# FFN up products from the fifth step on: one 512-column matmul for the weights' high half against both halves of the operand

## The reference

```python
def swiglu(h, w13, w2):
    gate, up = jnp.split(h @ w13, 2, axis=-1)
    return (jax.nn.silu(gate) * up) @ w2
...
        x = x + 0.5 * swiglu(rms_norm(x, ffn1_norm[l]), ffn1_w13[l], ffn1_w2[l])
...
        x = x + 0.5 * swiglu(rms_norm(x, ffn2_norm[l]), ffn2_w13[l], ffn2_w2[l])
```

## Time and profile before

| | |
|---|---|
| median of three runs | 1532.71 us (1531.86 to 1532.9) |
| the profiled execution | 1531.94 us, its span 1530.2 us |
| TensorE matmuls | 1494.6 us busy (98%), 11618 instructions |
| VectorE | 1164.2 us busy (76%), 1645 instructions |
| ScalarE | 788.5 us busy (52%), 1135 instructions |
| POOL | 115.6 us busy (8%), 71 instructions |
| DMA | 311.02 MB, 203 GB/s over the span |

### The profile page before, as it was taken

One profiled execution on the slowest core, in us unless ns is written; L12 is line 12 of the kernel. 1 busy time (PEld: TensorE's weight loads), 2 busy tenths in 40 slices (PEclk: granted clock), 3 DMA queues, 4 the chain that ended last, 5 costly groups with the idle time before them and its releaser, 6 DMA issues.

```text
span 1530.2 us, 28532 instructions
## 1 busy us (share of the span) xinstructions
PE 1494.6 (98%) x11618; PEld 1436.2 (94%) x11618; DVE 1164.2 (76%) x1645; ACT 788.5 (52%) x1135; POOL 115.6 (8%) x71
## 2 busy tenths in 40 slices
PE   7999999999999999999989999999999999899998
PEld 7999998999999899999769999987699999899998
DVE  7887788888877868887767876774778987785564
ACT  6534458654435644445765443454654544564442
POOL 0013000000200102110000100000000111000000
PEclk9999999999999999999999999999999999999999
DMA  7676752646675547675232867643345887345540
GB/s 271 244 256 235 250 218 84 246 172 244 236 259 192 220 158 283 243 252 220 84 138 111 303 244 251 247 148 137 104 152 216 303 283 255 128 149 217 186 166 28
DMA packets 44566, 311.02 MB, mean 203 GB/s; under 512 B 5744, under 2 KB 6000, under 8 KB 7344
## 3 DMA queue, kind: packets, MB, share of 16 engines
q1 hardware_dynamic: 42048, 303.33, 54.5%
q0 software_dynamic: 1840, 5.20, 1.1%
q10 hardware_dynamic: 576, 1.05, 0.2%
HBM read 308.46 MB, written 1.05 MB: 202 GB/s over the span
## 4 chain that ended last, share of the span: by engine, by line
PE 77%; DVE 3%; ACT 1%; issue 0%; DVEq 0%; ACTq 0%
PE psum L1860 21%; PE psum L1866 21%; PE psum L1867 21%; PE psum L2065 3%; PE psum L2071 3%; PE psum L2070 3%; DVE w_lo L1072 1%; PE psum L2382 1%; PE psum L2393 0%; PE psum L2312 0%; PE psum L2277 0%; PE psum L2184 0%; ACT w_hi L515 0%; DVE buf L1579 0%; PE psum L2232 0%
## 5 line engine op out<-in xcount | busy, mean ns | idle before, releaser
L1860 PE MATMUL psum<-u_hi,w_hi 128*128 128x256 f32 (+1 forms) x2288 | 654.9, 286 | 18.2 <-DVE u_lo L1169 9.7
L1072 DVE TENSOR_TENSOR w_lo<-raw,w_hi 128x1024 fp32r<-128x1024 f32 x480 | 593.9, 1254 | 93.4 <-ACT w_hi L515 93.2
L1866 PE MATMUL psum<-u_lo,w_hi 128*128 128x256 f32 (+1 forms) x2288 | 648.8, 284 | 0.0
L1867 PE MATMUL psum<-u_hi,w_lo 128*128 128x256 f32 (+1 forms) x2288 | 648.6, 283 | 0.0
L515 ACT ACTIVATE w_hi<-raw 128x1024 fp32r<-128x1024 f32 x480 | 488.4, 1047 | 73.6 <-PE psum L1860 58.7
L1860 PEld LDWEIGHTS psum<-u_hi,w_hi 128*128 128x128 f32 x2288 | 439.2, 192 | 22.8 <-DVE w_lo L1072 9.9
L1866 PEld LDWEIGHTS psum<-u_lo,w_hi 128*128 128x128 f32 x2288 | 439.4, 192 | 0.4
L1867 PEld LDWEIGHTS psum<-u_hi,w_lo 128*128 128x128 f32 x2288 | 439.3, 192 | 0.0
L1860 PE MATMUL psum<-hid_hi,w_hi 128*128 128x256 f32 x1220 | 346.0, 284 | 1.2 <-issue 1.2
L1866 PE MATMUL psum<-hid_lo,w_hi 128*128 128x256 f32 x1220 | 345.2, 283 | 0.0
L1867 PE MATMUL psum<-hid_hi,w_lo 128*128 128x256 f32 x1220 | 345.2, 283 | 0.0
(11 more groups left out here) (258 smaller groups left out, 1017.9 us busy)
## 6 DMA issues: line engine op xcount, KB each, us to landing
raw<-stream SPq DMA_DIRECT2D x288, 1024.0 KB, 4.8
buf<-tab POOLq DMA_DIRECT2D x2, 768.0 KB, 5.2
x<-x_in SPq DMA_DIRECT2D x2, 512.0 KB, 7.0
buf<-ctx_in POOLq DMA_DIRECT2D x1, 1024.0 KB, 7.1
buf<-poolmat POOLq DMA_DIRECT2D x1, 1024.0 KB, 5.3
out<-x ACTq DMA_DIRECT2D x4, 256.0 KB, 2.6
buf<-late POOLq DMA_DIRECT2D x1, 640.0 KB, 4.6
buf<-poolmat POOLq DMA_DIRECT2D x1, 512.0 KB, 8.0
```

The lines of the kernel that those rows point to most:

```text
L1072: ve.tensor_tensor(w_lo[:, u], raw[:, u], w_hi[:, u].bitcast(F32), ALU.subtract).then_inc(S.lo_ready, 1)
L1860: ins = te.matmul(dst, w_hi[:, w], hi, start=first, stop=False, skip_group_check=True)
L1866: te.matmul(dst, w_hi[:, w], lo, start=False, stop=False, skip_group_check=True)
L1867: return te.matmul(dst, w_lo[:, w], hi, start=False, stop=last, skip_group_check=True)
```

## The change

From step 4 on (`PLAIN = 4`) the up product of a unit is written by `wide_k` in place of `all_k`. `u_hi` and `u_lo` are now two halves of one buffer, and one matmul streams both, 256 columns each, past the chunk of `w_hi`: the sums with `u_hi` go to columns 0 to 255 of a bank, those with `u_lo` to columns 256 to 511. The matmul of `w_lo` with `u_hi` adds to columns 0 to 255. Three matmuls of 256 columns become one of 512 and one of 256. Gate and up have a bank each, and so the steps take banks 4 and 5 or 6 and 7 in turn. ScalarE copies the second halves of both banks to SBUF (`low_sums`), VectorE adds them to the first halves (`up_added`), and then multiplies by the norm factor, now from SBUF. `up(j)` waits for `up_added` of step j - 2. Steps 0 to 3, all down products and all other products are as before, and the columns streamed are the same in number.

```diff
+PLAIN = 4
-UP_BANK = [4, 5, 7, 6] + [4 + _j % 2 for _j in range(4, FFS)]
+UP_BANK = [4, 5, 7, 6] + [4 + 2 * (_j % 2) for _j in range(PLAIN, FFS)]
...
-        u_hi_t = sb("u_hi", NC * 2 * T, F32R)
-        u_lo_t = sb("u_lo", NC * 2 * T, F32R)
+        u_t = sb("u", 2 * NC * 2 * T, F32R)
...
+        u_both = u_t[:, :].rearrange("p (h k t) -> p h k t", h=2, k=NC)
+        u_hi, u_lo = u_both[:, 0], u_both[:, 1]
...
+        low_sums = buf5[:, 1024:1536].rearrange("p (k t) -> p k t", k=2)
...
                 def hidden(j, ahead=0):
 
+                    if j >= PLAIN:
+                        act.wait_ge(S.up_ready, h0 + j + 1)
+                        sc.activation(low_sums, psum[:, UP_BANK[j]:UP_BANK[j] + 2, T:2 * T], ACT.Copy).then_inc(S.up_copied, 1)
                     act.wait_ge(S.up_scaled, h0 + j + 1)
...
                     dve.wait_ge(S.up_ready, h0 + j + 1)
-                    ve.tensor_tensor(t2.rearrange("p (k t) -> p k t", k=2), bank2(UP_BANK[j]), over2(rstd[:, :]),
-                                     ALU.mult).then_inc(S.up_scaled, 1)
+                    b, both = UP_BANK[j], t2.rearrange("p (k t) -> p k t", k=2)
+                    if j < PLAIN:
+                        ve.tensor_tensor(both, bank2(b), over2(rstd[:, :]), ALU.mult).then_inc(S.up_scaled, 1)
+                    else:
+                        wide = FFN_AT[name] * (FFS - PLAIN) + j - PLAIN + 1
+                        dve.wait_ge(S.up_copied, wide)
+                        ve.tensor_tensor(both, psum[:, b:b + 2, 0:T], low_sums, ALU.add).then_inc(S.up_added, 1)
+                        dve.wait_ge(S.up_added, wide)
+                        ve.tensor_tensor(both, both, over2(rstd[:, :]), ALU.mult).then_inc(S.up_scaled, 1)
...
+            def wide_k(c, i, bank):
+
+                unit_ready(c, i)
+                for k in range(NC):
+                    w = slice((c % RING) * UNIT + k * P, (c % RING) * UNIT + (k + 1) * P)
+                    ins = te.matmul(bank2(bank), w_hi[:, w], u_both[:, :, k, 0:T], start=k == 0, stop=False, skip_group_check=True)
+                    if k == 0:
+                        ins.then_inc(S.unit_used, 1)
+                        begun[0] = c
+                    ins = te.matmul(bank2(bank)[:, 0, :], w_lo[:, w], u_hi[:, k, 0:T], start=False, stop=k == NC - 1, skip_group_check=True)
+                return ins
+
+            def wide_up(c, i, j, bank, h0, a0):
+
+                if not isinstance(j, int) or j > PLAIN + 1:
+                    pe.wait_ge(S.up_added, a0 + j - PLAIN - 1)
+                else:
+                    pe.wait_ge(S.up_scaled, h0 + j - 1)
+                wide_k(c, i, bank)
+                wide_k(c + 1, i, bank + 1).then_inc(S.up_ready, 1)
...
-                for j in range(4, 10):
-                    up(unit_at(name, "up", j), 0, j, UP_BANK[j], h0)
+                for j in range(PLAIN, 10):
+                    wide_up(unit_at(name, "up", j), 0, j, UP_BANK[j], h0, a0)
                     down(j - 2, (j - 2) % 4, unit_at(name, "down", j - 2))
...
-                        up(c, 2 * i, j, 4 + s % 2, h0)
+                        wide_up(c, 2 * i, j, UP_BANK[10 + s], h0, a0)
```

More of the change, by code:

```diff
@@ L157 @@
 I_UNITS = [AT["gates"] + _n for _n in (5, 7)]
+FFN_AT = {f"ffn{_n}": _n for _n in range(4)}
 STEPS = {"ffn0": 0, "ffn1": FFS, "ffn2": 2 * FFS, "ffn3": 3 * FFS, "mlp0": 4 * FFS, "mlp1": 4 * FFS + MLS}
@@ L195, in __init__ @@
         self.up_scaled = sem("up_scaled")
+        self.up_copied = sem("up_copied")
+        self.up_added = sem("up_added")
         self.gated = sem("gated")
@@ L339, in build @@
         x = x_t[:, :].rearrange("p (k t) -> p k t", k=NC)
-        u_hi = u_hi_t[:, :].rearrange("p (k t) -> p k t", k=NC)
-        u_lo = u_lo_t[:, :].rearrange("p (k t) -> p k t", k=NC)
-        u_hif = u_hi_t[:, :].bitcast(F32).rearrange("p (k t) -> p k t", k=NC)
+        u_both = u_t[:, :].rearrange("p (h k t) -> p h k t", h=2, k=NC)
+        u_hi, u_lo = u_both[:, 0], u_both[:, 1]
+        u_hif = u_t[:, 0:NC * 2 * T].bitcast(F32).rearrange("p (k t) -> p k t", k=NC)
         hid_hi = hid_hi_t[:, :].rearrange("p (s t) -> p s t", s=2)
@@ L1933, in up @@
                 all_k(c + 1, i, bank2(bank)[:, 1, :]).then_inc(S.up_ready, 1)
+            def wide_k(c, i, bank):
[15 more added lines that the diff above has]
+                wide_k(c + 1, i, bank + 1).then_inc(S.up_ready, 1)
             def swiglu(name, norm, free=lambda: None):
-                c0, h0 = AT[name], STEPS[name]
+                c0, h0, a0 = AT[name], STEPS[name], FFN_AT[name] * (FFS - PLAIN)
                 def down(j, slot, c, i=0, first=False, last=False):
```

## The result

The changed kernel takes 1524.51 us, the median of five runs (1524.29 to 1525.42), against 1532.79 us (1531.86 to 1533.5) before. The ratio is 0.9948, with a 95% interval of 0.9937 to 0.996: it is faster, by 8.3 us and not by the 15.4 that were forecast. The time lies above the stated range of 1513.5 to 1522. Its profiled execution took 1525.42 us, the slowest of the five, with a span of 1523.4.

A forecast was written before the change was run, and what follows sets the result against it. The prediction took TensorE's matmul stream as the bound: 1152 matmuls fewer at 13.3 ns make 15.4 us less, all other terms cost 0, so 1531.94 us becomes 1516.6, with 0.8 for the median 1517.3 us. Range 1513.5 to 1522.

The forecast's parts named there:

- What bounds the kernel: Steps 4 to 21 of the four FFNs: only TensorE's stream counts, 8.64 us a step, while VectorE stays inside that.
- What a wider matmul costs: Up products: 226.7 ns for 512 columns against 240.0 for two of 256, so 13.3 ns for each matmul fewer.
- The rule of 2.5 ns: Trainium skill's isolated gap, N/2.4 + 2.5 ns: a matmul fewer saves 2.5 ns, the change 2.9 us.
- TensorE's matmuls: Up products of steps 4 to 21: 1152 triples become pairs, 13.3 ns less each, 15.4 us less in sum.
- ScalarE's copy and VectorE's add: Behind each up product, 72 times each: copy 0.60 us, add 0.69, delaying what follows by at most 1.37 us, hidden.
- The margin: Fullest steps, step 6 of ffn0: VectorE's added work still fits before the next add, with 0.23 us to spare.
- The end of an FFN: Step 21: the last two splits on VectorE end later but ahead of the residual update, 0.3 us left, cost 0.
- The banks: An up product takes two banks; its wait for the add of two steps before costs 0.
- Rivals 1 and 4: Up products: the pair takes 360 ns, no gain, 1532.7 us; chances 5% and 2%.
- Rival 2: Fullest steps: VectorE becomes the bound, 4.4 us lost in ffn0 and in ffn1, time 1526; chance 6%.
- Rival 3: Wide matmuls: an operand from two places is read at a lower rate, 219 us slower at 430 ns; chance 3%.
- rival 1: Wide matmul: its second half starts like a matmul of its own, 240 ns, no gain, 1532.7 us; chance 5%.

The follow-up runs named there:

- e5: The changed kernel, but the second matmul of each chunk is wide as well (w_lo with u_hi and u_lo, 512 columns): 1641.86 us in one run.
- e8: The changed kernel, but each step issues both units' sixteen wide matmuls first and then the sixteen narrow ones: 1519.34 us, ratio 0.9914.
- e7: The changed kernel, but each unit issues two wide matmuls, then two narrow ones, four times: 1519.47 us, ratio 0.9914.
- e3: The changed kernel with its copy, add and banks, but the wide matmul issued as two of 256 columns: 1532.63 us, ratio 1.0002 to before.
- e1: The changed kernel, but the wide matmul reads one contiguous run of 512 columns of a constant buffer: 1524.64 us, ratio 0.995.
- e6: The changed kernel reordered to eight wide, then eight narrow matmuls a unit, the narrow ones with 128 columns in place of 256: 1514.12 us in one run.
- e9: The changed kernel, wide and second matmul in single turns, but the second one has 384 columns in place of 256: 1592.78 us in one run.
- e10: The changed kernel, but with two wide, two second matmuls in turns and 384 columns in the second ones: 1592.4 us in one run.
- e14: The changed kernel, but wide and 384-column matmuls in single turns both read one contiguous run of a constant buffer: 1592.25 us in one run.

## Why the prediction was wrong

- *What bounds the kernel*: right. TensorE was not idle in these steps, and in all orders of the table the time followed the price of the pair.
- *What a wider matmul costs*: this step failed. It took 346.7 ns for the pair, which is 226.7 for the wide and 120.0 for the narrow matmul, and got 353.0. Both prices are right for a settled stream (e5, e8), but with single turns the stream never settles. All of the missing 6.3 ns are the "wide matmul that takes turns with a narrow one", which the text names as not shown by the rows. The trace of the kernel before did hold a hint. The earlier trace rows begins with the tenth wide matmul after a pause. 5.3 us earlier, wide matmuls of the same projection follow directly behind narrow ones:

```profile
483.72 0.28 PE L1867 MATMUL psum<-hid_hi,w_lo 128*128 128x256 f32 x1
483.84 0.40 PE L2065 MATMUL psum<-w_hi,u_hi 128*128 128x512 f32 x1
...
485.47 0.39 PE L2070 MATMUL psum<-w_lo,u_hi 128*128 128x512 f32 x1
```

Seven distances in 1.63 us are 233 ns each, above the 0.230 us at which the forecast's own range ends. With 120.0 they give the measured 353.0. That it fits so well is partly luck, since the same sum would hold for e7, which took 348.3. The text kept 240 as the upper bound, and the pair's effective wide price, 353.0 - 120.0 = 233 ns, is half-way. But it gave its own forecast a range of 0.224 to 0.230 and left everything beyond to a rival with 5%. The bounds should have stayed in the range.
- *The rule of 2.5 ns* from the Trainium skill ("TensorE: Matmul & The Clock Gate", section "Back-to-back issue gap") would have given 1529.8 us, too high by 5.3; mine was too low by 7.2. Settled streams of either width have 13.3 ns besides the columns, so the rule isn't borne out. The same section's sustained 131 ns for 512 columns isn't either: 226.7.
- *TensorE's matmuls*: the count of 1152 was right, the sum 15.4 us was 7.3 too large at 7.0 ns for each in place of 13.3.
- *ScalarE's copy and VectorE's add*: right. The timeline of VectorE in step 5 of ffn0 and at the start of step 6, beside the earlier trace rows:

```profile
56.76 0.69 DVE L1260 TENSOR_TENSOR buf<-psum,buf 128x512 f32<-128x512 f32 x1 [0.85 <-ACT buf L583]
57.48 0.69 DVE L1262 TENSOR_TENSOR buf<-buf,rstd 128x512 f32<-128x512 f32 x1
...
62.23 2.73 DVE L1088 SCALAR_TENSOR_TENSOR buf<-raw,tiny,buf 128x512 f32<-128x512 f32 x4
65.28 0.69 DVE L1260 TENSOR_TENSOR buf<-psum,buf 128x512 f32<-128x512 f32 x1 [0.33 <-ACT buf L583]
```

The add holds VectorE from 56.76 to 57.48, 0.72 us (0.73 priced), and the steps are 8.52 to 8.53 apart. The margin is the 0.33 in the brackets: 0.23 as worked out, plus the 0.10 by which the period came out longer. The new groups, ACT's copy and VectorE's two:

```profile
L583 ACT ACTIVATE buf<-psum 128x512 f32<-128x512 f32 x72 | 42.9, 596 | 121.8 <-PE psum L1958 121.7
```
```profile
L1262 DVE TENSOR_TENSOR buf<-buf,rstd 128x512 f32<-128x512 f32 x72 | 60.0, 833 | 2.5
L1260 DVE TENSOR_TENSOR buf<-psum,buf 128x512 f32<-128x512 f32 x72 | 49.7, 690 | 54.9 <-ACT buf L583 54.6
```

Copy and add have 596 and 690 ns, as priced. The multiply has 833, not 690: 10.3 us more over the 72, which is why VectorE is busy for 1224.0 us and not for the 1214 forecast. That I had not seen; the last section shows where it comes from. VectorE is late by it in some steps, and the lead of the weights covers that, as the text had it for lateness of another origin.
- *The end of an FFN*: right. It left 0.33 us, and the brackets show 0.27. VectorE's timeline there, beside the earlier trace rows:

```profile
196.34 2.35 DVE L1079 TENSOR_TENSOR w_lo<-raw,w_hi 128x1024 fp32r<-128x1024 f32 x2
198.96 1.41 DVE L1194 SCALAR_TENSOR_TENSOR x<-psum,x 128x512 f32<-128x512 f32 x2 [0.27 <-PE psum L1881]
```

- *The banks*: right, nothing waited for them, and e3 measures all of the hidden part together at 0 (ratio 1.0002).
- *The rivals*: none came true. Rivals 1 and 4 had a pair of 360 ns, and it took 353.0. Rival 2 had VectorE as the bound: some steps ran late, but TensorE never ran short of weights. Rival 3 named addresses, and e1 and e5 show that they cost nothing. The truth lay between forecast and rival 1.

## What to carry to other kernels

Where TensorE is the bound, one 512-column matmul in place of two of 256 saves 13.3 ns once the stream has settled, and 7.0 to 12.1 ns in the mixtures tried here. So if it must mix with narrower ones, try the order of issue as a parameter of its own: the same matmuls took from 347.9 to 353.0 ns a pair. A price read from a uniform stream isn't the price in a mixed one. Read the distances at the edge of the stream too, where it follows another width, and where no row shows the mixture, keep both bounds in the range. To learn whether cover work is really hidden, run the change without its benefit, as e3 does.

## What the runs showed of the hardware

- **Spacing by width**, each with its own load of 128x128 fp32r weights, at the full granted clock: 112 to 114 ns for 128 columns (e6), 120.0 for 256 (e3), 226.7 for 512 once settled (e5), and 186 for 384 if the wide one beside it keeps its 226.7 (e9, e10, e14). 384 lies off the line of its neighbours, and no run here says why.
- **A wide stream starts dear.** Behind narrow matmuls the first five distances are 233, 236, 228, 232 and 231 ns and all further ones 226.7 (e5 and e8, the same in all 72 steps within 1 ns or so). In the kernel before, a pause of TensorE of 0.85 us has the same behind it: from the second wide start after it, at 487.28, six distances take 1.39 us, 232 ns each, and then come 226.7.
- **The order** of 512- and 256-column matmuls changes the pair's price by up to 5 ns, repeatably (the 72 steps of a run agree within 0.01 us). It depends on none of: operand in one or two places, half of the bank, bank, weight buffer. The cause stays open.
- **VectorE's multiply from SBUF is held up by POOL's sums.** The changed kernel's VectorE and POOL around a group sum:

```profile
82.34 0.69 DVE L1260 TENSOR_TENSOR buf<-psum,buf 128x512 f32<-128x512 f32 x1 [0.32 <-ACT buf L583]
83.07 1.83 DVE L1262 TENSOR_TENSOR buf<-buf,rstd 128x512 f32<-128x512 f32 x1
...
91.07 0.68 DVE L1260 TENSOR_TENSOR buf<-psum,buf 128x512 f32<-128x512 f32 x1
```
```profile
82.12 3.23 POOL L454 PARTITION_ALL_REDUCE mod_row<-buf  x1 [66.59 <-DVE buf L1088]
```

While POOL reduces (82.12 to 85.35), the add that reads PSUM runs in 0.69 us, and the multiply with two SBUF inputs takes 1.83 in place of 0.69. The next step then starts without a wait, late. In the changed kernel 15 of the 72 multiplies are longer than the rest, by up to 1.64 us, and all of these end 0.44 to 0.47 us before the recorded end of a reduction, whenever they began. The kernel before had it too, in another place. Its multiply read PSUM: 22 of the 88 ran while POOL reduced, and none took more than 0.69. But 17 of its 480 w_lo splits, which read two SBUF operands and mostly take 1.22 us, took 1.5 to 3.0, all of them while POOL worked and fifteen during a reduction:

```profile
853.05 2.98 DVE L1072 TENSOR_TENSOR w_lo<-raw,w_hi 128x1024 fp32r<-128x1024 f32 x1
```
```profile
852.72 3.22 POOL L450 PARTITION_ALL_REDUCE mod_row<-buf  x1 [145.64 <-DVE buf L1081]
```

So the longer multiply could have been forecast from the trace of before.

The Trainium skill ("SBUF — State Buffer", section "SBUF: two separate sides") says that a VectorE instruction with two SBUF inputs and a GpSimd one that reads SBUF share a port pair, which one of them holds for its whole instruction. The trace agrees in the main: up to 1.64 us more on the SBUF form, none on the PSUM form. But the hold is shorter than POOL's recorded time, which is rough: the multiply that began at 83.07 was over at 84.90, and the reduction at 85.35. Both kinds fit a hold that ends 1.14 us before the recorded end: multiplies of 0.69 us then end 0.45 before it, and splits of 1.22 us end 0.08 after it, as 14 of the fifteen above do to 0.01 us.
